# Expert weights in longer pieces, a final norm for each tile, and hidden rows turned inside the next block's products

## The reference

```
lg    = xf @ w_group + b_group          # 4 groups of 8 experts; each row takes one group
el    = xf @ w_router + b_router        # and in it the TOP_K = 2 best of 8 experts
hid_e = silu(x_e @ w_gate[e]) * (x_e @ w_up[e])     # 32 experts, 1024 -> 512, twice
y_e   = hid_e @ w_down[e]                           # 512 -> 1024
x     = x + mod_x[5] * sum over the 2 experts of weight * y_e
out   = x * rsqrt(mean(x * x) + EPS) * final_g
```

## Time and profile before

| what | us |
|---|---|
| median of three runs (lowest, highest) | 2198.43 (2194.53, 2198.77) |
| the profiled execution: its own time | 2196.42 |
| the profiled execution: its span | 2194.7 |
| PE busy in it | 2023.5 (92%) |
| DVE, ACT, POOL busy | 836.5, 293.9, 359.7 |
| first product of the first expert block to the last of the last down | 1608.8 to 2172.9 |

### The profile page before, as it was taken

One profiled execution on the slowest core, in us unless ns is written; L12 is line 12 of the kernel. 1 busy time (PEld: TensorE's weight loads), 2 busy tenths in 40 slices (PEclk: granted clock), 3 DMA queues, 4 the chain that ended last, 5 costly groups with the idle time before them and its releaser, 6 DMA issues.

```text
span 2194.7 us, 20943 instructions
## 1 busy us (share of the span) xinstructions
PE 2023.5 (92%) x8189; PEld 1134.5 (52%) x8189; DVE 836.5 (38%) x1456; ACT 293.9 (13%) x544; POOL 359.7 (16%) x387
## 2 busy tenths in 40 slices
PE   5999999999999999999999999999887888897575
PEld 3433334444446864687555599997432333333232
DVE  3488856011430242013695144545232332221124
ACT  2100000000210001102212243330200000000001
POOL 1344431000000000000000357640021111111020
PEclk9999999999999999998999999999999999999798
DMA  6221212313344444521110899616289999999994
GB/s 225 77 77 39 77 39 77 115 39 115 102 153 141 152 153 153 185 77 39 39 53 1 350 411 408 268 39 230 83 298 380 342 383 382 384 388 383 357 365 180
DMA packets 180476, 425.61 MB, mean 194 GB/s; under 512 B 9304, under 2 KB 26013, under 8 KB 180253
## 3 DMA queue, kind: packets, MB, share of 16 engines
q1 hardware_dynamic: 165408, 393.86, 48.8%
q0 software_dynamic: 8192, 22.16, 2.8%
q10 hardware_dynamic: 6781, 8.27, 1.1%
HBM read 335.83 MB, written 88.43 MB: 193 GB/s over the span
## 4 chain that ended last, share of the span: by engine, by line
PE 88%; issue 4%; DMA 4%; DVE 2%; ACT 1%; DVEq 0%; SPq 0%; POOLq 0%; ACTq 0%; POOL 0%
PE pb L572 51%; PE pb L1643 12%; PE pb L802 10%; PE pb L1657 5%; DMA arena<-in_w_gate_dram 3%; PE pb L715 2%; PE pb L2151 1%; PE pb L2163 1%; PE pb L1637 1%; PE pb L808 1%; ACT arena L563 1%; PE pb L1712 1%; DMA arena<-in_x_dram 1%; PE pb L604 0%; PE pb L1650 0%
## 5 line engine op out<-in xcount | busy, mean ns | idle before, releaser
L572 PE MATMUL pb<-arena 128*128 128x512 f32 (+1 forms) x3072 | 1084.0, 515 | 9.5 <-DVE arena L2544 3.1
L572 PEld LDWEIGHTS pb<-arena 128*128 128x128 f32 x3072 | 583.6, 191 | 505.4 <-issue 462.6
L1643 PE MATMUL pb<-arena 128*64 128x512 f32 x1216 | 295.1, 641 | 62.7 <-issue 57.6
L1643 PEld LDWEIGHTS pb<-arena 128*64 128x64 f32 x1216 | 107.9, 147 | 243.9 <-issue 243.9
L802 PE MATMUL pb<-arena 128*128 128x128 f32 x2016 | 232.0, 277 | 0.9 <-DVE arena L1342 0.9
L802 PEld LDWEIGHTS pb<-arena 128*128 128x128 f32 x2016 | 229.1, 193 | 2.4 <-DVE arena L1342 1.3
L1515 POOL TENSOR_TENSOR arena<-arena,sm 128x512 f32<-128x512 f32 x12 | 12.3, 1042 | 898.2 <-DMA arena<-decay_rows 898.2
L1657 PE MATMUL pb<-arena 128*64 128x512 f32 x608 | 138.8, 597 | 19.8 <-issue 18.7
L1796 DVE TENSOR_TENSOR arena<-pb,sm 128x512 f32<-128x512 f32 x38 | 26.3, 691 | 297.3 <-PE pb L1637 290.9
L2605 DVE SCALAR_TENSOR_TENSOR arena<-pb,st,arena 128x256 f32<-128x256 f32 x32 | 15.5, 483 | 249.7 <-PE pb L572 249.7
L1594 POOL DMA_DIRECT2D expert_rows<-arena x68 | 34.9, 514 | 379.6 <-issue 345.1
(11 more groups left out here) (420 smaller groups left out, 1433.7 us busy)
## 6 DMA issues: line engine op xcount, KB each, us to landing
expert_rows<-arena SPq DMA_DIRECT2D x6, 12288.0 KB, 77.1
arena<-in_w_gate_dram SPq DMA_DIRECT2D x32, 2048.0 KB, 20.4
arena<-in_w_up_dram SPq DMA_DIRECT2D x32, 2048.0 KB, 20.4
arena<-in_w_down_dram SPq DMA_DIRECT2D x32, 2048.0 KB, 20.6
arena<-in_w_in_dram SPq DMA_DIRECT2D x16, 2048.0 KB, 8.0
arena<-in_w_ff_dram SPq DMA_DIRECT2D x16, 2048.0 KB, 8.3
arena<-in_w_mod_dram SPq DMA_DIRECT2D x12, 2048.0 KB, 12.9
arena<-in_w_out_dram SPq DMA_DIRECT2D x4, 2048.0 KB, 10.9
```

Source lines behind the costliest of these rows:

```text
L572: l = nc.tensor.matmul(o, lhs[i], rhs[i], start=(i == 0), stop=(i == n - 1))
L1643: l = nc.tensor.matmul(PB[2 + s][64 * h:64 * h + 64, :].rearrange("p (g n) -> p g n", g=2), XG[s][:, k % 4, 64 * (k // 4):64 * (k // 4) + 64],
```

## The change

There are four parts. **Weights:** gate and up are loaded as `(p k) n -> p k n`, so that partition p holds features 8p to 8p + 7, a run of 16 KB that is contiguous on both sides; down as `(h q c) n -> q h c n`, a run of 8 KB for each half. All that is multiplied with them is permuted alike: `xm` is written permuted and read strided from `res`, the transposes of `logits` and the vectors of `-gs` read with a step of eight elements (`by_eight`), the router's weights are loaded permuted, and the gated product writes its result with even and odd columns apart. The bytes and the number of DMAs stay the same.

**Turns:** the two transposes of the hidden rows of block n - 1 are issued after half of the products of `gate_up(n)`, and no longer ahead of `down(n - 1)`. On ACT the copy of the hidden rows of block n - 1 goes ahead of the tanh of block n.

**The last block:** its gate products are issued when gate has landed (8 × 2 products of 256 columns), then the turn of the block before, and then the up products.

**The final norm:** the first two of the late products start when the first half of the last block's result is copied. ACT loads the table of the square root ahead of the norm and takes the root of each tile; VectorE takes the sums and the scalings in the order sum 0, sum 1, scale 0, sum 2, scale 1, sum 3, scale 2, scale 3.

```diff
+        by_eight = lambda x: x.rearrange("p (q c) -> p c q", c=KD)
...
             for i in range(16):
-                l = nc.tensor.matmul(PB[g % 4][:, i:i + 1], modb[:, D + P * i:D + P * i + P], ident[:, 0:1], start=True, stop=True)
+                vec = by_eight(modb[:, D * (1 + i // KD):D * (2 + i // KD)])[:, i % KD]
+                l = nc.tensor.matmul(PB[g % 4][:, i:i + 1], vec, ident[:, 0:1], start=True, stop=True)
...
-                        l = nc.tensor.transpose(PB[g % 4][:, c * P:(c + 1) * P], res[:, k, (4 * i + c) * P:(4 * i + c + 1) * P], ident)
+                        l = nc.tensor.transpose(PB[g % 4][:, c * P:(c + 1) * P], by_eight(res[:, k])[:, 4 * i + c], ident)
...
         def sp_experts(sp):
             names3 = ("w_gate_2", "w_up_2", "w_down_2")
-            unit_src = lambda m, e: (a[names3[m]][0][e] if isinstance(e, int) else a[names3[m]][0][bass.ds(e, 1)].rearrange(
-                "o d n -> (o d) n")).rearrange("(k p) n -> p k n", p=P)
-            slot_view = lambda i, m: at(W_SLOT[i], 16).rearrange("p (k n) -> p k n", k=8 if m < 2 else 4)
+            one = lambda m, e: a[names3[m]][0][e] if isinstance(e, int) else a[names3[m]][0][bass.ds(e, 1)].rearrange(
+                "o d n -> (o d) n")
+            unit_src = lambda m, e: (one(m, e).rearrange("(p k) n -> p k n", p=P) if m < 2 else
+                                     one(m, e).rearrange("(h q c) n -> q h c n", h=2, c=2))
+            slot_view = lambda i, m: (at(W_SLOT[i], 16).rearrange("p (k n) -> p k n", k=KD) if m < 2 else
+                                      at(W_SLOT[i], 16).rearrange("p (h c n) -> p h c n", h=2, c=2))
...
-            def gate_up_rows(i, s):
+            def gate_up_rows(i, s, halfway=None):
                 for k in range(KD):
+                    if halfway and k == KD // 2:
+                        halfway()
                     for h in range(2):
...
                                              slot_pair(i, k, h), start=(k == 0), stop=(k == KD - 1))
+                return l
+
+            def gate_or_up_rows(i, s, m):
+                w = at(W_SLOT[(3 * i + m) % 8], 16).rearrange("p (k n) -> p k n", k=KD)
+                o = 0 if gate_first(i) == (m == 0) else 256
+                for k in range(KD):
+                    for h in range(2):
+                        l = nc.tensor.matmul(PB[2 + s][64 * h:64 * h + 64, o:o + 256],
+                                             XG[s][:, k % 4, 64 * (k // 4):64 * (k // 4) + 64],
+                                             w[:, k, 256 * h:256 * h + 256], start=(k == 0), stop=(k == KD - 1))
                 return l
...
-            def gate_up(n):
+            def gate_up(n, halfway):
 
                 i, s = BLOCKS[n][0], n % 2
                 slot_loaded(pe, 3 * i)
-                slot_loaded(pe, 3 * i + 1)
                 pe.wait_ge(sem("e_xg"), n + 1)
                 if n >= 2:
                     pe.wait_ge(sem("e_hid"), n - 1)
-                gate_up_rows(i, s).then_inc(sem("e_gu"), 1)
-
-            def down(n):
-
-                i, s = BLOCKS[n][0], n % 2
+                if n < NBLK - 1:
+                    slot_loaded(pe, 3 * i + 1)
+                    gate_up_rows(i, s, halfway).then_inc(sem("e_gu"), 1)
+                else:
+                    gate_or_up_rows(i, s, 0)
+                    halfway()
+                    slot_loaded(pe, 3 * i + 1)
+                    gate_or_up_rows(i, s, 1).then_inc(sem("e_gu"), 1)
+
+            def hidden_turned(n):
+
                 pe.wait_ge(sem("e_hid"), n + 1)
                 if n >= 2:
                     pe.wait_ge(sem("e_htc"), n - 1)
-                turn_hidden(s).then_inc(sem("e_ht"), 1)
+                turn_hidden(n % 2).then_inc(sem("e_ht"), 1)
+
+            def down(n):
+
+                i, s = BLOCKS[n][0], n % 2
                 slot_loaded(pe, 3 * i + 2)
...
                 for n in range(a0, b0):
-                    gate_up(n)
+                    gate_up(n, (lambda: hidden_turned(n - 1)) if n > a0 else None)
                     if n + 1 < b0:
                         turn(n + 1)
                     if n > a0:
                         down(n - 1)
+                hidden_turned(b0 - 1)
                 down(b0 - 1)
...
-            pe.wait_ge(sem("e_copied"), NBLK)
-            for k in range(KT):
-                for h in range(2):
-                    l = nc.tensor.matmul(PB[2 * k + h][:], GP[:, k * P:(k + 1) * P], YP[:, h], start=True, stop=True)
-                l.then_inc(sem("late_pe"), 1)
+            pe.wait_ge(sem("e_copied"), NBLK - 1)
+            pe.wait_ge(sem("late_half"), 1)
+            for k, h in ((0, 0), (1, 0), (0, 1), (1, 1), (2, 0), (2, 1), (3, 0), (3, 1)):
+                if (k, h) == (0, 1):
+                    pe.wait_ge(sem("e_copied"), NBLK)
+                l = nc.tensor.matmul(PB[2 * k + h][:], GP[:, k * P:(k + 1) * P], YP[:, h], start=True, stop=True)
+                if h:
+                    l.then_inc(sem("late_pe"), 1)
...
             for a0, b0 in SEGMENTS:
                 for n in range(a0, b0):
                     if n == 1:
-                        tanh(n)
                         act.wait_ge(sem("scattered"), 16 * 2 * KT)
                         act.dma_start(fgb, a["final_g_2"].rearrange("(o d) -> o d", o=1).to_broadcast([P, D])).then_inc(
                             sem("fgb_loaded"), 16)
-                    else:
-                        tanh(n)
                     if n > a0:
                         turned_hidden(n - 1)
+                    tanh(n)
...
             def hidden_up(s, o):
-                return STT(HB[s], TB[s], 0.5, PB[2 + s][:, 256 - o:512 - o], ALU.mult, ALU.mult)
+                pairs = lambda x: x.rearrange("p (q c) -> p c q", c=2)
+                return STT(HB[s].rearrange("p (c q) -> p c q", c=2), pairs(TB[s]), 0.5, pairs(PB[2 + s][:, 256 - o:512 - o]),
+                           ALU.mult, ALU.mult)
...
-                    do(TT(YP[r, 0], PB[6 + s][0:32], G2[0:32], ALU.mult))
+                    if n < NBLK - 1:
+                        do(TT(YP[r, 0], PB[6 + s][0:32], G2[0:32], ALU.mult))
+                    else:
+                        TT(YP[r, 0], PB[6 + s][0:32], G2[0:32], ALU.mult).then_inc(sem("late_half"), 1)
                     TT(YP[r, 1], PB[6 + s][64:96], G2[64:96], ALU.mult).then_inc(sem("e_copied"), 1)
...
             for k in range(KT):
-                nc.scalar.activation(xm[k], res[:, k], ACT.Copy, scale=st[:, 4, k:k + 1]).then_inc(sem("xm_ready"), 1)
+                nc.scalar.activation(xm[k].rearrange("p (c q) -> p c q", c=KD), by_eight(res[:, k]), ACT.Copy,
+                                     scale=st[:, 4, k:k + 1]).then_inc(sem("xm_ready"), 1)
...
             act_experts(act)
+            act.wait_ge(sem("eps_ready"), 1)
+            nc.scalar.activation(st[:, 6, 0:1], st[:, 7, 0:1], ACT.Sqrt).then_inc(sem("roots"), 1)
+            act.wait_ge(sem("roots"), NORM["n6"] + 1)
             for k in range(KT):
-                act.wait_ge(sem("x3_sum"), k + 1)
+                act.wait_ge(sem("x3_sum"), 2 * k + 2)
                 nc.scalar.activation(at(144, 4), res[:, k], ACT.Square, accum_out=st[:, 0, k:k + 1]).then_inc(
                     sem("squares"), 1)
                 act.wait_ge(sem("squares"), SQUARES["n6"] + k + 1)
-            act_root(act, KT, "n6")
+                nc.scalar.activation(st[:, 3, k:k + 1], st[:, 0, k:k + 1], ACT.Sqrt, scale=1.0 / D,
+                                     bias=st[:, 7, 0:1]).then_inc(sem("roots"), 1)
...
+            V.memset(st[:, 7, 0:1], EPS).then_inc(sem("eps_ready"), 1)
             dve_experts(dve, do, between)
-            for k in range(KT):
+            def late_sum(k):
+
                 dve.wait_ge(sem("late_pe"), k + 2)
-                do(TT(res[:, k, 0:512], res[:, k, 0:512], PB[2 * k][:], ALU.add))
+                TT(res[:, k, 0:512], res[:, k, 0:512], PB[2 * k][:], ALU.add).then_inc(sem("x3_sum"), 1)
                 TT(res[:, k, 512:1024], res[:, k, 512:1024], PB[2 * k + 1][:], ALU.add).then_inc(sem("x3_sum"), 1)
-            dve_rstd(dve, ch, KT, D, "n6")
+
+            def scaled_out(k):
+
+                dve.wait_ge(sem("roots"), NORM["n6"] + k + 2)
+                do(V.reciprocal(st[:, 4, k:k + 1], st[:, 3, k:k + 1]))
+                STT(res[:, k], res[:, k], st[:, 4, k:k + 1], fgb, ALU.mult, ALU.mult).then_inc(sem("x3_ready"), 1)
+
             dve.wait_ge(sem("fgb_loaded"), 16)
-            for k in range(KT):
-                STT(res[:, k], res[:, k], st[:, 4, k:k + 1], fgb, ALU.mult, ALU.mult).then_inc(sem("x3_ready"), 1)
+            late_sum(0)
+            late_sum(1)
+            for k in range(2, KT):
+                scaled_out(k - 2)
+                late_sum(k)
+            scaled_out(2)
+            scaled_out(3)
...
-            wr_src = lambda w: a[w][0].rearrange("(k p) n -> p k n", p=P)
+            wr_src = lambda w: a[w][0].rearrange("(p k) n -> p k n", p=P)
```

## The result

The changed kernel takes **2170.48 us** (median of 4 runs, 2169.58 to 2177.08) against 2198.6 of the kernel before (4 runs beside it, 2194.53 to 2199.05): ratio **0.9883**, 95% interval 0.986 to 0.9905. It is 28 us faster; the forecast was 38.

The account below looks back on a forecast made before the run. Weight bytes set the pace over 387 us, with PE between and a plain chain last. Terms -27.1 - 6 - 3.3 - 3 + 1 = -38.4 us take the profiled 2196.4 to 2158.0, 2160 us as median; range 2146 to 2184.

Parts of the forecast that it names:

- What bounds the kernel: Whole kernel: weight bytes set the pace over 387 us, PE does between, and the end is a plain chain.
- A: Weight loads: longer pieces raise the middle stage from 384 to 413.5 GB/s, -27.1 us (ends 13.9 and 36.6 saved).
- the factor 0.975: Middle stage: measured 384 GB/s over the 394 that pieces alone give, applied to 424 to get 413.5 GB/s.
- G: Transposes and `-gs` products on PE reading with a 32-byte step: +1 us, between nothing and 7.8 us.
- D: Last block: gate products start 5 us earlier, at gate's landing, -6 us (between -4.5 and -6.8).
- E: Final norm: VectorE goes without rest and the table load is hidden, -3.3 us (between -2.5 and -4).
- F: Turns inside the next block's products: 0.52 us idle goes, switch costs 0 to 0.5; ten blocks gain, -3 us (-5 to 0).
- H: Row transfers on POOL's queue beside 16 KB weight pieces: three gathers take 18.5 us; put at 0, at worst +5 us.
- Rival 1: Weight loads: longer pieces bring nothing, held by DRAM at 384 GB/s or cut to 2 KB; 2187 us, chance 0.12.
- Rival 2: Weight loads: new address order is slower, deciding under about 372 GB/s; at 346 GB/s 2225 us, chance 0.08.

Follow-up runs that it names:

- e1: The kernel before with the new order of the weights (longer pieces) and the strided operands it needs, nothing else: 2180.92 us, ratio 0.9913.
- e11: The changed kernel storing only a quarter of the result rows of 64-row blocks and half of those of 32-row blocks: 2163.07 us, ratio 0.9839.
- e12: The kernel of e11, with no more than 16 rows loaded too from the ninth block on: 2150.9 us, ratio 0.9788.
- e5: The changed kernel run again without any edit: 2170.73 us, ratio 0.988.
- e2: The kernel before with only the turns of hidden rows moved into the middle of the next block's products: 2194.04 us, ratio 0.9985.
- e4: The kernel before with only the final norm's new order of late products, sums, roots and scalings: 2194.39 us, ratio 0.9987.
- e7: The changed kernel with gate and up in pieces of 4 KB, operands strided by 8 bytes: 2170.71 us, ratio 0.988.
- e9: The changed kernel with the `-gs` vectors turned by 16-row transposes, the kernel of e6 run again: 2166.32 us, ratio 0.9861.
- e3: The kernel before with only the last block's gate products issued when gate has landed: 2191.92 us, ratio 0.997.
- e6: The changed kernel with the 32 one-column products of `-gs` replaced by 16 transposes of 16 rows: 2162.43 us, ratio 0.9847.
- e10: The kernel of e9 with the sixth add of gathered rows moved behind the last block's gated product: 2163.21 us, ratio 0.9841.

## Why the prediction was right, and where it was not

**What bounds the kernel** was right. Transfers run without a rest from 1750 to 2050 us (share 1.01), PE waits for up, and what shortens the weights shortens the time: e1 brings more than the three other parts together.

**A, longer pieces: mechanism right, size off.** Forecast 413.5 GB/s and -27.1 us. Over 140 us the changed kernel runs at 395, and only where blocks have 32 rows or fewer at 412 to 417. What failed is the factor 0.975, taken from the kernel before and carried over as if it were a property of the mix. Where blocks are small it held: 415 is 0.98 of the 424 GB/s that the pieces alone gave in the sum. Where most blocks are full it is 395 / 424 = 0.93. In the kernel before the two stretches differ by 1% (383 and 387), here by 5% (395 and 415). Fewer stores alone change nothing (e11), fewer loads on top of them bring 4% (e12): the difference goes with the loads of the rows. The sum also had too many rows: four blocks of three experts do not all have 64 rows, and from 1760 to 1900 us POOL's queue moves 4.37 of 55.32 MB, 8% and not 10%, in packets of 4 KB and not 2; put right, this moves the forecast pace by less than 1 GB/s. In the sum A is -20 us (e1: -19.8; e5, which has the turns too: -23.5), inside the range that was given, -13.9 to -36.6. Of the 20 us, 4 KB pieces give most: with them blocks 0 to 36 took 15.9 us less, with 16 KB ones, turns in both, 19.3 to 23.5 (five profiles, mean 21.8).

**G, strided operands: the term that was most wrong.** +1 us was taken because a record of one column takes about as long as one of 128, "so the elements read are not what most of it is spent on". But both records stand on a weight load, and it is the load that reads the strided side. Its 192 ns became 335 and set the pace of the group: 3.63 us became 7.66, so this group alone doubled, as the upper end had it for both. The transposes, the other group, kept their 1.05 us for eight; their loads went from 140 to 191 ns and stay under 272 ns of product. The rest of the loss I had no term for: with the slow group came falls of the granted clock, in the first profile at 1511.1 us (6.8 us long) and 1552.0 (3.4), and one at 1589.6 that met the last logits. First the changed kernel, then the kernel before:
```profile
1513.25 16.28 PE L717 MATMUL pb<-arena 128*128 128x512 f32 x32
...
1552.37 15.50 PE L717 MATMUL pb<-arena 128*128 128x512 f32 x32
...
1590.81 3.63 PE L572 MATMUL pb<-rows,arena 128*128 128x36 f32 x16 [0.69 <-ACT arena L1913]
```
```profile
1509.16 13.98 PE L715 MATMUL pb<-arena 128*128 128x512 f32 x32
...
1582.58 1.98 PE L572 MATMUL pb<-rows,arena 128*128 128x36 f32 x16 [0.79 <-ACT arena L1880]
```
The two groups of wide products (L717) around the first two falls took 16.28 and 15.50 us where 13.98 stood, the last eight transposes 1.33 where 1.07 stood, and the logits behind them 3.63 where 1.98 stood. With the slow group itself that is 4.0 + 3.8 + 0.3 + 1.65 = 9.8 of the 10.2 us. Over all profiles, block 0 starts 7.4 us late on average in the six with a step of 16 or 32 bytes in `-gs` (+4.4 to +10.5), and 0.7 us early in the four with a turned `-gs` or a step of 8 bytes (-2.3 to +1.6); the four with the old order of weights lie at 0 to +2.9. That the clock falls because of the slow group is argued, not shown. In all six profiles with a slow group a fall of 6.8 us begins between 1508 and 1512 us. But in three of the eight with a quick one (e2, e4, e7) a fall of 3.4 us begins between 1505 and 1509, and e9 has one at 1539.5; the kernel before, e3, e6 and e10 have none between 1500 and 1579. So falls come there without the slow group too, shorter ones.

The scaling on ACT did take twice as long, as its worst case said, and stayed hidden. In the changed kernel:
```profile
1591.10 8.27 ACT L1919 ACTIVATE arena<-arena,st 128x1024 f32<-128x1024 f32 x4 [0.24 <-DVE st L1301]
...
1601.62 0.20 ACT L1924 ACTIVATE tk<-tk 128x4 f32<-128x4 f32 x1 [0.72 <-DVE tk L1968]
```
The earlier trace rows had 4.27 us, and with a step of 8 bytes (e7) it is 4.51. What the prediction named as the one waiting for it, the first picks, was not the closest: the routing's softmax on ACT (L1922, L1924) stands behind it, and of its 3.07 us of slack in the kernel before 0.72 are left, 0.28 in e5.
The Trainium skill (Advanced Engine Details and Errata, Memory Cachelines) says that full pace in SBUF needs two hits on each 16-byte line. Here 4 and 8 bytes of step (two or more elements of 4 bytes in a line) took 192 and 196 ns a load and 4.27 and 4.51 us on ACT; 16 and 32 bytes (one) took 329 and 335 ns and 8.13 and 8.27 us: the runs agree, to the place of the step. By this rule the forecast would have been 2167, closer than 2160; that it comes so close is partly luck, since its sum doubles the transposes too, which kept their time, and has no term for the clock.

**D, the last block** was right: -6.2 and -6.3 in the changed kernel, -6.5 alone (forecast -6). Loads of the 256-column products stay hidden: 3.67 us for the half of a block. It hides two parts that cancel, though: with the turn in the products it is worth 1.6 us more (e10: -7.9), and the gather takes that away. So part of the agreement is luck.

**E, the norm** was right: -3.8 in both profiles (forecast -3.3). VectorE goes nearly without rest, and ACT is late for 0.4 us once and for 0.15 at the end.

**F, the turns:** 0.29 us a block, inside the 0 to 0.5 for the switch; but where ten blocks were counted as keeping it, blocks 0 to 36 kept 1.1 us, about four blocks' worth: between the two early waits too, the next wait takes what was gained. With the last block e2's profile has 3.3 us, the forecast's 3. That is luck: 2.2 of them come from a place that the forecast did not count. In the company of the longer pieces how much of it is left is not shown.

**H, rows beside the weights:** put at 0, with +5 at the worst. It is not 0. The gathers did land in up to 17.1 us (estimate 18.5), and that they "have a block's spacing" did not save them: the adds are in VectorE's order ahead of the last gated product. It costs 1.4 us on PE there. The other half, row loads that slow the weights, was not in the list at all, and is the larger one: the step of A above.

**The rivals.** Rival 1 (the pieces bring nothing) falls with 395 to 417 GB/s against 383 to 387, and pieces of 16 KB go whole, as the packets show. Rival 2 (the order of addresses is slower) falls with the same rows; the 372 GB/s from which it decides stood in no 25 us between 1750 and 2050.

What stays open: why loads of 64 rows hold 16 KB pieces back when stores of as many don't. For blocks of 64 rows both go out on POOL's queue in packets of 4 KB. In e11, where only loads have such packets, they took 202 ns in the mean from 1760 to 1900 us; in the changed kernel loads and stores together took 176. Full stores with short loads were not run, and no experiment separates the reading in DRAM from the writing to the 64 partitions. And why runs of one kernel lie in two groups 6 us apart (e9: 2161.83, 2163.87, 2168.95, 2168.77) is not explained.

## What to carry to other kernels

A pace measured for one piece size in pure traffic says what the pieces allow; the factor between it and the mixed stage is not a constant, and the stage must be split by what else moves (here by the rows of a block) before it is carried over. When a layout makes an operand strided, look which side of the product reads it and whether that side is already the longer one: the same step was free in transposes and doubled a group of one-column products. Where an in-order engine waits for a transfer, a longer piece on the other queues moves that wait; put what the critical engine needs ahead of it.

## What the runs showed of the hardware that was not expected

- Weight loads of 128 x 128 f32 in plain products: 192 ns at a step of 4 bytes, 196 at 8, 329 at 16, 335 at 32. In transposes the loads went from 140 ns to 191 (step 32), 211 (step 16) and 209 (step 8): there the step's size doesn't decide.
- ScalarE's scaling of 128 x 1024 f32, four in a row: 4.27 us with a step of 4 bytes, 4.51 with 8, 8.13 with 16, 8.27 with 32.
- Pace by the length of the pieces of gate and up, beside the same rows: 383 GB/s with 2 KB, 391 with 4 KB, 399 with 8 KB and 392 to 395 with 16 KB; with few rows beside them 387, 404, 409 and 411 to 415.
- Transfers of another queue pay for them: a row load of 128 KB lands in 5.9 us beside 2 KB pieces, 6.7 beside 4 KB, 7.6 beside 8 KB and 8.6 to 9.0 beside 16 KB. The Trainium skill (DMA: Bandwidth & Descriptors, Queues, rings and completion order) says that an engine goes round its queues a whole packet of descriptors at a time; the order of these four agrees, their sizes follow from no figure there.
